# Square sums of 16 norms on four 32-column groups of the array, with their roots taken as rows

## The chip, the cores and the metric

The kernel runs on one core of a Trainium2 chip. The metric is the device time of one execution in microseconds; the kernel before took 1970.17 us (median of 3 runs, 1969.05 to 1970.89). One further execution was profiled. Engine names are those of the profile: PE is the matrix engine (PEld its weight loads), DVE, ACT and POOL are the vector, activation and general engines, SP issues the DMAs.

## The reference

A trunk of two layers over 1024 latent tokens of 1024 channels, with a context of 256 tokens. Layer 0 mixes tokens by a bidirectional recurrent block, layer 1 by a two-dimensional pooling mixer; each mixer is followed by a gated FFN with a convolution. Before and after each of these four blocks stands a norm over the channels of each token:

```python
def _rms_norm(x, g):
    xf = x.astype(jnp.float32)
    y = xf * lax.rsqrt(jnp.mean(xf * xf, axis=-1, keepdims=True) + EPS)
    return (y * g.astype(jnp.float32)).astype(x.dtype)
# per layer, latent stream:
h = _modulate(_rms_norm(x, norm_pre_mix[i]), sh_m, sc_m);  y = mixer(h)
x = x + g_m * _rms_norm(y, norm_post_mix[i])
f = _conv_ffn(_modulate(_rms_norm(x, norm_pre_ffn[i]), sh_f, sc_f), ...)
x = x + g_f * _rms_norm(f, norm_post_ffn[i])
```

So there are eight norms of the latent stream, four in each layer.

## The kernel before, in words

Everything lives transposed: channels on the 128 partitions in 8 tiles (KT), tokens along the free axis in two halves h of 512. The big products are made in three matmuls each, of high and low parts of both operands (line 803 and the lines 1221, 1249 and 1269 of the FFNs, which multiply two by two blocks with seven products and run in loops of ten steps); the two FFN loops fill most of the time. The order of each engine's work is written out by hand, and semaphores tie the engines together; an engine works strictly through its own list.

The norms are numbered q = 0 to 7 (even: before a mixer or FFN, odd: after it) and made for each half h, so there are 16. One norm goes like this:

1. ACT squares the eight channel tiles of a half (`square`). DVE or POOL add some of the squared tiles up beforehand (`chain_sums`, `even_sum`, `odd_sum`, `line_sums`); how many are left for PE is set by `form` and `chain_end`.
2. PE sums over the channels (`square_sums`, `direct_sums`, which call `column_sums`). For each of the four blocks t of 128 tokens the squares are the weights (128x128) and a column of ones streams past them, so the sums come out as columns, token on partition. The norms listed in `WIDE` stream 128 columns of ones instead of one, with 128 equal columns of sums. The calls per norm are (0,h): 1; (1,0): 1; (1,1): 2; (2,0): 1; (2,1): 4; (3,0): 1; (3,1): 3; (4,0): 5; (4,1): 1; (5,0): 1; (5,1): 4; (6,0): 4; (6,1): 5; (7,0): 1; (7,1): 3, in all 38.
3. ACT takes the root of the 128x4 sums into `rms` (`norm_root`).
4. DVE takes the reciprocal into `rstd` (`norm_scale`), four columns for each half.
5. PE spreads `rstd` over the partitions with four products against the identity (`spread`, not for q = 4, whose columns are used directly by `z_scale`), and DVE multiplies tiles by it from PSUM (`scale_tiles`, `gate`).

The norms 0 lie in the start, 1 and 2 around the second half of the first mixer's output product (`first_pair(0, ...)`), 3 at the end of the first FFN (`down_last`), 4 among the products with the pooling map (`z_tile`), 5 and 6 among and after the window sums and in `first_pair(1, ...)`, 7 at the end. PE's list puts other matmuls between steps 2 and 5, so that ACT and DVE have time for the root and the reciprocal:

```python
if (m, k) == (1, 3):
    square_sums(1, 0)
if (m, k) == (1, 7):
    spread(1, 0)
```

Of the kernel before, what the change touches and what calls it, by code (L numbers as in the profile page):

```python
# [19 lines left out]
P = 128  # L20
D = 1024
T = 1024
NC_ = 256
KT = D // P
# [42 lines left out]
FR = LINE / 1024  # L67
# [7 lines left out]
def build_trunk(nc, xT, ctxT, params, ada, wA, wB, wC, gatew, poolw, poolcnt, ident_in, outT):  # L75
    with ExitStack() as top:
# [7 lines left out]
        def overlay(*plan):  # L84
# [31 lines left out]
        ident = sb("ident", [P, P])  # L116
        ones = sb("ones", [P, P])
        eps = sb("eps", [P, 1])
        rms = sb("rms", [P, KT])
        rstd = sb("rstd", [P, KT])  # L120
        rms_c = sb("rms_c", [P, 2])
        rstd_c = sb("rstd_c", [P, 2])
# [9 lines left out]
            ("Hc_hi", [P, KT, NC_], F32R), ("Hc_lo", [P, KT, NC_], F32R), ("RA1", [P, TA]),  # L132
            ("IB0", [P, TA]), ("IB1", [P, TA]), ("TH0", [P, TA]), ("TH1", [P, TA]), ("gw", [P, 4, P]))
        RA, IB, TH = (RA0, RA1), (IB0, IB1), (TH0, TH1)
        quad, red = overlay(128 + FR, ("quad", [P, 4, D]), ("red", [P, 4, P]))
        sp, Mc, cAc = overlay(144 + FR, ("sp", [P, 8, 2 * NH]), ("Mc", [P, ADA0]), ("cAc", [P, KT]))
        ada_part, ada_row = overlay(56, ("ada_part", [P, 2, 4, P]), 2, ("ada_row", [P, 4 * P]))
# [215 lines left out]
        sq_made, sum_even, sum_odd = ([sem(f"{n}{h}") for h in range(2)] for n in ("sq_made", "sum_even", "sum_odd"))  # L353
        sum_both, sum_last = ([sem(f"{n}{h}") for h in range(2)] for n in ("sum_both", "sum_last"))
        zmap_made, z_scaled = sem("z_map_made"), sem("z_scaled")
        ssq_done, rms_made = ([sem(f"{n}{h}") for h in range(2)] for n in ("ssq_done", "rms_made"))
        rstd_made, rb_done = ([sem(f"{n}{h}") for h in range(2)] for n in ("rstd_made", "rb_done"))
        csq_made, ctx_norm_step = sem("ctx_sq_made"), sem("ctx_norm_step")
        caffine, chi, hc_ready = sem("ctx_affine"), sem("ctx_hi"), sem("ctx_h_ready")
# [145 lines left out]

            return 2 if q in (3, 7) else 6 + h if q == 4 else 4 + h

        WIDE = ((2, 1), (3, 1), (4, 0), (5, 1), (6, 0), (6, 1), (7, 1))

        def ssq_out(q, h):  # L510

            bank = ps[:, ssq_bank(q, h)]
            return bank if (q, h) in WIDE else bank[:, 4 * h:4 * h + 4]

        def rb_bank(q, h):

# [281 lines left out]
        def _(pe):  # L798
# [60 lines left out]

            def column_sums(q, h, src, at, first, last):  # L860

                out, w = ssq_out(q, h), P if (q, h) in WIDE else 1
                for t in range(4):
                    mm = pe.matmul(out[:, t * w:t * w + w], src[:, at + t * P:at + t * P + P],  # L864
                                   ones[:, 0:w], start=first and t == 0, stop=last and t == 3)
                if last:
                    mm.then_inc(ssq_done[h], 1)

# [44 lines left out]
                    pe.wait_ge(sum_last[h], trees_to(q + 1, h))  # L913
                    column_sums(q, h, *total, True, True)

            def shift_map(half):

                bank = 5 - half
                if half == 0:
                    pe.wait_ge(poolw_full, 16)  # L920
                    pe.wait_ge(coef_ready, 4)
                pe.wait_ge(d_added, half_added("22", 0, PAIRS) + (16 if half else 13))
                for g in (2 * half, 2 * half + 1):
                    for k in range(2):
                        c = (g % 2) * 512 + k * 256
                        mm = pe.matmul(ps[:, bank, (g % 2) * 256:(g % 2) * 256 + 256],
                                       M[:, 48 + 2 * g + k:49 + 2 * g + k].to_broadcast([P, P]),
                                       pool_w[:, half, c:c + 256], start=k == 0, stop=k == 1)
                mm.then_inc(z_done, 1)

            def spread(q, h):
# [5 lines left out]
                                   start=True, stop=True)  # L937
                mm.then_inc(rb_done[h], 1)

            def norm(q, h):  # L940
                square_sums(q, h)
                spread(q, h)


            def ada_rows(g, ks, units=slice(0, 4)):

# [36 lines left out]
            pe.wait_ge(const_full, 16)  # L983
            square_sums(0, 0)
            row_columns(0, 1, ada_cols)
            spread(0, 0)
            pe.wait_ge(ada_first_full[2], 32)
            ada_rows(1, range(KT))
# [17 lines left out]
            pe.wait_ge(ctx_norm_step, 5)  # L1006
            square_sums(0, 1)
            row_columns(3, 3, ada_out)
            first_pieces(0, pairs((4,)))
            spread(0, 1)  # L1010
            first_pieces(0, pairs((5, 6, 7)))
# [87 lines left out]
            for m in range(KT):  # L1099
                s, n = "AB"[m % 2], NH + REPEATED + m // 2  # L1100
                pe.wait_ge(w_ready[s], n + 1)
                pe.wait_ge(y_evac, m + 1 if m < 4 else m + 5)
                for k in range(KT):
                    if m == 0:
                        wait_gated(1, k)
                    if (m, k) == (1, 1):
                        pe.wait_ge(y_evac, KT)
                        ada_columns(4 * NH, 4, ps[:, 7, 0:4])
                    if (m, k) == (1, 3):
                        square_sums(1, 0)  # L1110
                    if (m, k) == (1, 7):
                        spread(1, 0)
                    if (m, k) == (5, 5):
                        square_sums(2, 0)
                    if (m, k) == (6, 1):
                        spread(2, 0)
                    mm = product(s, k * P, [(ps[:, m % 4], H_hi[:, k, hs(1)], H_lo[:, k, hs(1)])],
                                 k == 0, k == KT - 1)
                mm.then_inc(unit_done[s], 1)
# [33 lines left out]
            def down_last(L):  # L1153
# [21 lines left out]
                for n in range(6, 2 * KT):  # L1175
                    if n == KT:
                        pe.wait_ge(last_ready, 2 * L + 2)
                    pe.wait_ge(d_added, added + n - 5)
                    half_tile(n, False)
                    half_tile(n, True).then_inc(d_done, 1)  # L1180
                    if n == 8 and L == 0:
                        quad_columns(PAIRS + 1, ps[:, 3, 0:4])
                    if n == 10:
                        square_sums(q, 0)
                    if n == 11:
                        spread(q, 0)
                if L == 0:
                    shift_map(0)
                    square_sums(q, 1)
                    shift_map(1)  # L1190
                    spread(q, 1)
                else:
                    old_x(0, added + 12)
                    square_sums(q, 1)
                    old_x(2, added + 13)
                    spread(q, 1)
                    old_x(4, added + 14)
                    old_x(6, added + 15)
                    for m in TAIL_BANK:
                        plus_gated(m)  # L1200
# [81 lines left out]
            def first_pair(L, h):  # L1282
# [6 lines left out]
                for (s, banks), k in order:  # L1289
# [7 lines left out]
                    if (L, h, s) == (0, 0, "A"):  # L1297
                        if k == 0:
                            pe.wait_ge(y_evac, KT + 5)
                        if k == 3:  # L1300
                            square_sums(1, 1)
                        if k == 5:
                            spread(1, 1)
                    if (L, h, s, k) == (1, 0, "A", 4):
                        spread(5, 1)
                    if (h, s) == (0, "C"):
                        if (L, k) == (0, 0):
                            cols_and_second()
                        if (L, k) == (1, 2):
                            direct_sums(6, 1, KT - 2)  # L1310
                        if k == 3:
                            direct_sums(2 + 4 * L, 1, begin=KT - 2 if L else None)
                            square_sums(2 + 4 * L, 1, direct=False)
                        if k == 5:
                            spread(2 + 4 * L, 1)
                    mm = product(s, k * P, [piece(banks, H_hi, H_lo, k, h)], k == 0, k == KT - 1)
# [25 lines left out]

            ffn(0)

            def z_tile(i):

                b = 2 * (i % 3)
                if i == 0:
# [5 lines left out]
                for g in range(4):  # L1354
                    for k in range(2):
                        if i % 4 == 0:
# [2 lines left out]
                        mm = pe.matmul(ps[:, b + g // 2, (g % 2) * 256:(g % 2) * 256 + 256],  # L1359
                                       X[:, 2 * g + k, i * P:i * P + P], pool_s[:, g // 2, c:c + 256],  # L1360
                                       start=k == 0, stop=k == 1)
                mm.then_inc(z_done, 1)

            def window_sums(n):

                h, mt = n // KT, BOX_TILES[n]
                g, out = mt // 2, ps[:, n % 4]
# [20 lines left out]
                tiles.sort(key=lambda i: rows(i) != (8 * h, 8 * h + 8))  # L1388
                covered = 8 * h
                for i in tiles:  # L1390
                    r0, r1 = rows(i)
                    if n == 0 and i == KT - 1:
                        pe.wait_ge(zt_lo, KT)
# [14 lines left out]

            z_tile(0)
            square_sums(4, 0)  # L1410
            for i in range(1, 5):
                z_tile(i)
            square_sums(4, 1)
            for i in range(5, KT):
                z_tile(i)
            for n in range(2 * KT):
                window_sums(n)
                if n == 10:
                    square_sums(5, 0)
                if n == 11:  # L1420
                    spread(5, 0)
            square_sums(6, 0)
            spread(6, 0)
            square_sums(5, 1)
            ffn(1)
# [3 lines left out]
        def _(act):  # L1429
# [56 lines left out]

            def norm_root(q, h):
                act.wait_ge(ssq_done[h], q + 1)
                sums = ssq_out(q, h)
                if (q, h) in WIDE:  # L1490
                    sums = sums.rearrange("p (t c) -> p t c", t=4)[:, :, 0]
                A(rms[:, 4 * h:4 * h + 4], sums, ACT.Sqrt, scale=1.0 / D,
                  bias=eps[:, 0:1]).then_inc(rms_made[h], 1)

            def fill_h(i, L, ffn_part, h, ks=range(KT)):

# [918 lines left out]
        def _(dve):  # L2415
# [38 lines left out]

            def norm_scale(q, h):
                c = slice(4 * h, 4 * h + 4)
                dve.wait_ge(rms_made[h], q + 1)
                if q:
                    dve.wait_ge(rb_done[h], spreads_to(q))
                dve.reciprocal(rstd[:, c], rms[:, c]).then_inc(rstd_made[h], 1)  # L2460

            def ada_sum(i):

# [758 lines left out]
```

## Time and profile before

| | us |
|---|---|
| median of 3 runs | 1970.17 |
| profiled execution | 1970.25 |
| its span in the profile | 1968.4 |
| PE busy (98% of the span) | 1936.0 |
| DVE busy (85%) | 1664.5 |
| POOL busy (65%) | 1275.9 |
| ACT busy (51%) | 994.8 |

Matmuls overlap in the records: the time from one start to the next is what PE spends, not the length of a record. The profiled execution's time is 1.85 us longer than its span, which begins and ends with the first and last recorded work.

### The profile page before, as it was taken

Reading aid. Unit: us, or ns where it says so; the run is one execution under the profiler, and the core shown is the slowest. Engines: PE = TensorE matmul, PEld = TensorE weight load, DVE = VectorE, ACT = ScalarE, POOL = GpSimd, SP = SyncE. Lnnn points to the kernel's source line nnn. Section 1 sums busy time; section 2 is a strip of 40 time slices with the busy share of each in tenths; the row PEclk is TensorE's granted clock in tenths of the full one; section 3 lists DMA queues with packets and bytes.
Section 4 is the critical chain, followed back from the end, with each engine's and each line's share of the span. In section 5 each row is a group of like instructions: output and inputs, shape, how many; then the busy total and the mean of one; then the engine's idle time right before and its main releaser. Section 6 shows DMA issues by size and latency. Waiting matters only on the chain.

```text
span 1968.4 us, 28040 instructions
## 1 busy us (share of the span) xinstructions
PE 1936.0 (98%) x8830; PEld 1575.5 (80%) x8830; DVE 1664.5 (85%) x1760; ACT 994.8 (51%) x1423; POOL 1275.9 (65%) x856
## 2 busy tenths in 40 slices
PE   7999999999999999999999999999999999999999
PEld 3777777788888888888888789878888888888886
DVE  5588888878889898899889886897888888888887
ACT  5767768466544444444444465663433334333434
POOL 3544234575877788977788985475577655556765
PEclk9999999999999999999999999999999999999999
DMA  8232322541222223222232241111111111111114
GB/s 332 89 104 85 123 81 91 203 160 45 87 85 96 96 85 96 81 89 96 85 96 96 67 179 40 69 64 45 63 53 53 54 53 64 53 53 57 50 53 181
DMA packets 78016, 179.74 MB, mean 91 GB/s; under 512 B 5104, under 2 KB 28944, under 8 KB 77328
## 3 DMA queue, kind: packets, MB, share of 16 engines
q1 hardware_dynamic: 77968, 179.13, 26.6%
q8 instruction: 27, 0.44, 0.1%
q14 instruction: 21, 0.17, 0.0%
HBM read 166.52 MB, written 12.58 MB: 91 GB/s over the span
## 4 chain that ended last, share of the span: by engine, by line
PE 87%; DVE 5%; ACT 4%; POOL 2%; issue 1%; DMA 1%; SPq 1%; ACTq 0%; POOLq 0%; DVEq 0%
PE ps L1249 40%; PE ps L1269 19%; PE ps L803 17%; PE ps L1054 3%; PE ps L1398 2%; PE ps L864 1%; PE ps L1221 1%; DMA ada_first<-ada 1%; PE ps L1359 1%; DVE Y L2526 1%; PE ps L935 0%; DVE X L2536 0%; PE ps L857 0%; POOL rawC L2119 0%; ACT RA L1619 0%
## 5 line engine op out<-in xcount | busy, mean ns | idle before, releaser
L2303 POOL TENSOR_TENSOR So_lo<-So_raw,So_hi 128x512 fp32r<-128x512 f32 x120 | 197.8, 1656 | 199.2 <-DVE So_raw L2955 168.1
L3019 DVE TENSOR_TENSOR Y<-Y,ps 128x1024 f32<-128x1024 f32 x280 | 324.3, 1211 | 3.1
L1822 ACT ACTIVATE So_hi<-So_raw 128x512 fp32r<-128x512 f32 x180 | 112.4, 625 | 145.6 <-POOL So_raw L2295 73.0
L2074 POOL TENSOR_TENSOR red<-red,E_quad 128x512 f32<-128x512 f32 x77 | 123.4, 1603 | 61.5 <-ACT E_quad L1876 58.7
L1822 ACT ACTIVATE WB_hi<-rawB 128x512 fp32r<-128x512 f32 x120 | 74.6, 629 | 165.9 <-PE ps L1249 111.8
L2027 POOL TENSOR_TENSOR WA_lo<-rawA,WA_hi 128x1024 fp32r<-128x1024 f32 x20 | 58.0, 2899 | 144.2 <-DVE u L2648 103.6
L1822 ACT ACTIVATE WA_hi<-rawA 128x512 fp32r<-128x512 f32 x120 | 73.1, 625 | 123.2 <-PE ps L1269 83.4
L1249 PE MATMUL ps<-T_hi,So_hi 128*128 128x512 f32 x336 | 131.2, 391 | 0.0
L1249 PE MATMUL ps<-T_hi,So_lo 128*128 128x512 f32 x336 | 130.8, 389 | 0.0
L1249 PE MATMUL ps<-T_lo,So_hi 128*128 128x512 f32 x336 | 130.7, 389 | 0.0
L1249 PE MATMUL ps<-H_hi,WA_hi 128*128 128x512 f32 x336 | 130.7, 389 | 0.0
L1249 PE MATMUL ps<-H_lo,WA_hi 128*128 128x512 f32 x336 | 130.7, 389 | 0.0
L1249 PE MATMUL ps<-H_hi,WA_lo 128*128 128x512 f32 x336 | 130.7, 389 | 0.0
L2303 POOL TENSOR_TENSOR WB_lo<-rawB,WB_hi 128x512 fp32r<-128x512 f32 x80 | 128.9, 1630 | 0.0
L2303 POOL TENSOR_TENSOR WA_lo<-rawA,WA_hi 128x512 fp32r<-128x512 f32 x80 | 105.5, 1319 | 3.8 <-ACT WA_hi L1822 3.8
L3007 DVE TENSOR_TENSOR Ub<-t,ps 128x512 f32<-128x512 f32 x84 | 57.8, 688 | 46.6 <-ACT t L1854 37.9
L1726 ACT ACTIVATE S<-S 128x1024 f32<-128x1024 f32 x46 | 48.8, 1061 | 92.6 <-DVE S L2864 92.6
L803 PE MATMUL ps<-H_hi,WA_hi 128*128 128x512 f32 x252 | 91.0, 407 | 4.2 <-POOL WA_lo L2027 1.6
L2858 DVE SCALAR_TENSOR_TENSOR S<-Ub,par,S 128x1024 f32<-128x1024 f32 x48 | 83.7, 1744 | 6.2 <-ACT S L1721 6.2
L3007 DVE TENSOR_TENSOR t<-t,ps 128x512 f32<-128x512 f32 x84 | 57.3, 682 | 36.2 <-PE ps L1249 36.2
L803 PE MATMUL ps<-H_hi,WA_lo 128*128 128x512 f32 x252 | 87.3, 393 | 0.0
L803 PE MATMUL ps<-H_lo,WA_hi 128*128 128x512 f32 x252 | 87.2, 392 | 0.0
(450 smaller groups left out, 6299.4 us busy)
## 6 DMA issues: line engine op xcount, KB each, us to landing
rawA<-wA SPq DMA_DIRECT2D x62, 512.0 KB, 3.3
rawB<-wB SPq DMA_DIRECT2D x62, 512.0 KB, 3.3
E_quad<-ada SPq DMA_DIRECT2D x44, 512.0 KB, 3.4
quad<-ada SPq DMA_DIRECT2D x8, 2048.0 KB, 9.3
rawB<-wC SPq DMA_DIRECT2D x22, 512.0 KB, 3.7
rawA<-wC SPq DMA_DIRECT2D x20, 512.0 KB, 3.7
ada_first<-ada SPq DMA_DIRECT2D x8, 1024.0 KB, 15.6
outT<-X SPq DMA_DIRECT2D x16, 512.0 KB, 3.0
```

Source lines behind the costliest of these rows:

```text
L803: mm = pe.matmul(out, w[:, w_cols:w_cols + P], (hi, lo)[part], start=first and w is W_hi[s] and part == 0, stop=last and w is W_lo[s])
L1054: mm = pe.matmul(out, gw[:, gi], src, start=True, stop=True)
L1249: mm = pe.matmul(ps[:, UP_OUT[name]], w[:, at + k * P:at + k * P + P], right[part][:, k], start=k == 0 and w is hi and part == 0, stop=k = ...
L1269: mm = pe.matmul(ps[:, DOWN_OUT[name][m]], w[:, at + m * P:at + m * P + P], TOKEN[name][part], start=name in ("11", "S1", "12") and w is h ...
L1726: A(S[0][:], S[0][:], ACT.Gelu_apprx_tanh).then_inc(gelu_done, 1)
L1822: A(dst[:, at:at + HF], op_source(name), ACT.Copy).then_inc(op_hi, 1)
L2027: TT(W_lo[s][:], raw[s][:], W_hi[s][:].bitcast(F32), ALU.subtract).then_inc(w_ready[s], 1)
L2074: TT(red[:], red[:], E_quad[:, :, k % 2 * P:k % 2 * P + P], ALU.add).then_inc(red_made, 1)
L2303: TT(lo[:, at:at + HF], op_source(name), hi[:, at:at + HF].bitcast(F32), ALU.subtract)\
L2858: STT(S[0][:], Ub[:, 0:T], col("ffn_conv_w", 72 * L + j), S[0][:], ALU.mult, ALU.add)\
L3007: TT(dst, a, b, op).then_inc(up_added, 1)
L3019: TT(at, at, ps[:, bank:bank + 2, :], ALU.add).then_inc(d_added, 1)
```

## The change

The roles of squares and ones are swapped. Of each call the four token blocks go to the four groups of 32 columns of the array: the weights are 32 columns of ones, the squares of the block stream past (128 columns), and the sums come out as a row, on the 32 partitions of the block's group (32 equal rows). ACT takes the root of the whole 128x128 tile into a new SBUF tile `rms_row`. One new product, `root_columns`, has `rms_row` as weights and four columns of the identity (0, 32, 64, 96) as the moving operand; it gives the four columns of roots in the same PSUM bank, and DVE's reciprocal reads them there. `WIDE` is gone: all norms are done alike. `root_columns` stands in PE's list between the sums and the spread of each norm, at places chosen one by one: between two k tiles, inside `shift_map`, `z_tile` or `window_sums` (through a new argument `between`), or straight after the sums. One semaphore for each half, `rms_step`, counts both the root and the product. The number of calls of `column_sums` is the same.

```diff
-        def ssq_out(q, h):
-
-            bank = ps[:, ssq_bank(q, h)]
-            return bank if (q, h) in WIDE else bank[:, 4 * h:4 * h + 4]
+        def ssq_rows(q, h):
+
+            return ps[:, ssq_bank(q, h), 0:P]
+
+        def rms_columns(q, h):
+
+            return ps[:, ssq_bank(q, h), P:P + 4]
...
             def column_sums(q, h, src, at, first, last):
 
-                out, w = ssq_out(q, h), P if (q, h) in WIDE else 1
                 for t in range(4):
-                    mm = pe.matmul(out[:, t * w:t * w + w], src[:, at + t * P:at + t * P + P],
-                                   ones[:, 0:w], start=first and t == 0, stop=last and t == 3)
+                    mm = pe.matmul(ssq_rows(q, h)[32 * t:32 * t + 32], ones[:, 0:32], src[:, at + t * P:at + t * P + P],
+                                   start=first, stop=last)
...
+            def root_columns(q, h):
+
+                pe.wait_ge(rms_step[h], 2 * q + 1)
+                pe.matmul(rms_columns(q, h), rms_row[:], ident[:].rearrange("p (t c) -> p t c", t=4)[:, :, 0],
+                          start=True, stop=True).then_inc(rms_step[h], 1)
...
             row_columns(0, 1, ada_cols)
+            root_columns(0, 0)
             spread(0, 0)
...
             row_columns(3, 3, ada_out)
+            root_columns(0, 1)
             first_pieces(0, pairs((4,)))
...
                     if (m, k) == (1, 3):
                         square_sums(1, 0)
+                    if (m, k) == (1, 5):
+                        root_columns(1, 0)
...
+                    if (m, k) == (5, 7):
+                        root_columns(2, 0)
...
                     half_tile(n, False)
+                    if n == 11:
+                        root_columns(q, 0)
                     half_tile(n, True).then_inc(d_done, 1)
...
                     square_sums(q, 1)
-                    shift_map(1)
+                    shift_map(1, lambda: root_columns(q, 1))
                     spread(q, 1)
                 else:
                     old_x(0, added + 12)
                     square_sums(q, 1)
+                    root_columns(q, 1)
                     old_x(2, added + 13)
...
                         if k == 3:
                             square_sums(1, 1)
+                        if k == 4:
+                            root_columns(1, 1)
                         if k == 5:
                             spread(1, 1)
+                    if (L, h, s, k) == (1, 0, "A", 2):
+                        root_columns(5, 1)
                     if (L, h, s, k) == (1, 0, "A", 4):
                         spread(5, 1)
...
+                        if k == 4:
+                            root_columns(2 + 4 * L, 1)
                         if k == 5:
                             spread(2 + 4 * L, 1)
...
             square_sums(4, 0)
-            for i in range(1, 5):
+            z_tile(1, lambda: root_columns(4, 0))
+            for i in range(2, 5):
                 z_tile(i)
             square_sums(4, 1)
-            for i in range(5, KT):
+            z_tile(5, lambda: root_columns(4, 1))
+            for i in range(6, KT):
                 z_tile(i)
             for n in range(2 * KT):
-                window_sums(n)
+                window_sums(n, (lambda: root_columns(5, 0)) if n == 11 else None)
...
             square_sums(6, 0)
+            root_columns(6, 0)
             spread(6, 0)
...
             def norm_root(q, h):
                 act.wait_ge(ssq_done[h], q + 1)
-                sums = ssq_out(q, h)
-                if (q, h) in WIDE:
-                    sums = sums.rearrange("p (t c) -> p t c", t=4)[:, :, 0]
-                A(rms[:, 4 * h:4 * h + 4], sums, ACT.Sqrt, scale=1.0 / D,
-                  bias=eps[:, 0:1]).then_inc(rms_made[h], 1)
+                A(rms_row[:], ssq_rows(q, h), ACT.Sqrt, scale=1.0 / D, bias=eps[:, 0:1]).then_inc(rms_step[h], 1)
...
-                dve.wait_ge(rms_made[h], q + 1)
+                dve.wait_ge(rms_step[h], 2 * q + 2)
                 if q:
                     dve.wait_ge(rb_done[h], spreads_to(q))
-                dve.reciprocal(rstd[:, c], rms[:, c]).then_inc(rstd_made[h], 1)
+                dve.reciprocal(rstd[:, c], rms_columns(q, h)).then_inc(rstd_made[h], 1)
```

## Rows read from the trace of the kernel before

**Rows 1.** The page: busy time of the engines, and the chain that ended last.
```profile
PE 1936.0 (98%) x8830; PEld 1575.5 (80%) x8830; DVE 1664.5 (85%) x1760; ACT 994.8 (51%) x1423; POOL 1275.9 (65%) x856
...
PE 87%; DVE 5%; ACT 4%; POOL 2%; issue 1%; DMA 1%; SPq 1%; ACTq 0%; POOLq 0%; DVEq 0%
```
**Rows 2.** The chain of waits from 380 to 470 us, then 1130 to 1300: shares by line.
```profile
by line: PE ps L803 82.1%; PE ps L864 7.6%; PE ps L935 4.0%; PE ps L850 1.5%; POOL H_lo L2038 1.5%; DVE Y L2512 0.8%; ACT H_hi L1501 0.8%; ACT H_hi L1505 0.7%; ACT Y L1503 0.7%; PE ps L1278 0.4%; issue 0.3%; ACTq L1498 0.0%
...
by line: PE ps L1398 18.8%; PE ps L803 10.3%; PE ps L1359 8.4%; PE ps L864 8.1%; issue 7.4%; PE ps L1380 3.6%; DVE X L2536 2.9%; DVE T_raw L2836 2.7%; DVE V L2423 2.6%; DVE T_raw L2838 2.5%; DVE Y L2526 2.4%; POOL X L2084 2.2%; ACT H_hi L15
```
**Rows 3.** PE's groups by shape, line 864: xcount | busy us, mean ns | idle before.
```profile
L864 PE MATMUL ps<-ones,sq 128*128 128x128 f32 x104 | 12.2, 276 | 0.0
...
L864 PE MATMUL ps<-ones,sq 128*128 128x1 f32 x32 | 3.7, 242 | 0.0
```
**Rows 4.** Windows of line 864: stretch and length, busy (xcount), granted clock, DMA share, GB/s.
```profile
0.00:1968.00 1968.00, 37.29 (x304) 1.00 0.27 91
...
1163.80:1168.34 4.54, 4.54 (x40) 4.51 (x39) 1.00 0.00 0
...
387.19:388.00 0.81, 0.81 (x8) 0.81 (x7) 1.00 0.00 0
```
**Rows 5.** PE's timeline around small products: start us, length us, line, operands, xcount [idle before].
```profile
440.36 0.39 PE L803 MATMUL ps<-H_hi,WB_lo 128*128 128x512 f32 x1
440.68 0.40 PE L1278 MATMUL ps<-ident,cnt_row 32*128 32x32 f32 x2
441.01 0.60 PE L850 MATMUL ps<-ones,red 128*128 128x1 f32 x4
...
36.34 4.45 PE L950 MATMUL ps<-ada_first,silu_c 128*2 128x512 f32 x10 [1.87 <-DMA ada_first<-ada]
40.73 0.50 PE L803 MATMUL ps<-H_hi,WA_hi 128*128 128x512 f32 x1
```
**Rows 6.** Windows of all engines: PE, PEld, DVE, ACT, POOL busy (xcount), then granted clock.
```profile
50.00:52.00 2.00, 0.52 (x3) 0.55 (x3) 0.74 (x1) 1.23 (x3) 1.93 (x2) 0.83 0.00 0
...
50.00:60.00 10.00, 8.52 (x35) 7.74 (x36) 6.28 (x11) 7.15 (x14) 7.45 (x6) 0.66 0.56 168
...
1234.00:1238.00 4.00, 4.00 (x37) 3.97 (x36) 3.30 (x6) 2.19 (x4) 3.55 (x3) 1.00 0.42 161
```
**Rows 7.** ACT's groups by shape: the roots, and a copy of 128x512 out of PSUM.
```profile
L1492 ACT ACTIVATE rms<-ps,eps 128x4 f32<-128x4 f32 x16 | 4.1, 258 | 23.4 <-PE ps L864 23.4
...
L1960 ACT ACTIVATE z_shift<-ps 128x512 f32<-128x512 f32 x2 | 1.2, 598 | 0.4 <-PE ps L926 0.4
```
**Rows 8.** Timeline of the norms (1,1) and (2,1), all engines.
```profile
431.15 0.18 DVE L2460 RECIPROCAL rstd<-rms 128x4 f32<-128x4 f32 x1 [0.35 <-ACT rms L1492]
...
445.06 0.69 DVE L2445 TENSOR_TENSOR sq<-ps,sq 128x512 f32<-128x512 f32 x1
...
447.40 0.27 ACT L1492 ACTIVATE rms<-ps,eps 128x4 f32<-128x4 f32 x1 [4.31 <-PE ps L864]
...
452.17 0.47 PE L803 MATMUL ps<-H_hi,WA_hi 128*128 128x512 f32 x1 [0.47 <-DVE H_lo L2518]
```
**Rows 9.** Timeline of the norms (3,1), (4,0), (5,0), (6,0) and (5,1), all engines.
```profile
1158.22 0.18 DVE L2460 RECIPROCAL rstd<-rms 128x4 f32<-128x4 f32 x1 [0.76 <-ACT rms L1492]
...
1165.55 1.74 POOL L2055 TENSOR_TENSOR sq<-sq 128x512 f32<-128x512 f32 x1
...
1220.12 0.24 ACT L1492 ACTIVATE rms<-ps,eps 128x4 f32<-128x4 f32 x1
...
1235.72 0.69 DVE L2445 TENSOR_TENSOR sq<-ps,sq 128x512 f32<-128x512 f32 x1
...
1245.66 0.18 DVE L2460 RECIPROCAL rstd<-rms 128x4 f32<-128x4 f32 x1 [0.51 <-ACT rms L1492]
```
**Rows 10.** Timeline of the tail, norm (7,1): DVE's adds and ACT's root.
```profile
1954.25 2.62 DVE L2536 TENSOR_TENSOR X<-X,Y 128x512 f32<-128x512 f32 x2
...
1956.52 0.26 ACT L1492 ACTIVATE rms<-ps,eps 128x4 f32<-128x4 f32 x1 [2.18 <-PE ps L864]
```

More of the change, by code:

```diff
@@ L118, in build_trunk @@
         eps = sb("eps", [P, 1])
-        rms = sb("rms", [P, KT])
+        sb("gap_rms", [P, KT])
         rstd = sb("rstd", [P, KT])
@@ L134, in build_trunk @@
         RA, IB, TH = (RA0, RA1), (IB0, IB1), (TH0, TH1)
+        rms_row, = overlay(145 + FR, ("rms_row", [P, P]))
         quad, red = overlay(128 + FR, ("quad", [P, 4, D]), ("red", [P, 4, P]))
@@ L355, in build_trunk @@
         zmap_made, z_scaled = sem("z_map_made"), sem("z_scaled")
-        ssq_done, rms_made = ([sem(f"{n}{h}") for h in range(2)] for n in ("ssq_done", "rms_made"))
+        ssq_done, rms_step = ([sem(f"{n}{h}") for h in range(2)] for n in ("ssq_done", "rms_step"))
         rstd_made, rb_done = ([sem(f"{n}{h}") for h in range(2)] for n in ("rstd_made", "rb_done"))
@@ L506, in ssq_bank @@
             return 2 if q in (3, 7) else 6 + h if q == 4 else 4 + h
-        WIDE = ((2, 1), (3, 1), (4, 0), (5, 1), (6, 0), (6, 1), (7, 1))
-        def ssq_out(q, h):
-            bank = ps[:, ssq_bank(q, h)]
-            return bank if (q, h) in WIDE else bank[:, 4 * h:4 * h + 4]
+        def ssq_rows(q, h):
+            return ps[:, ssq_bank(q, h), 0:P]
+        def rms_columns(q, h):
+            return ps[:, ssq_bank(q, h), P:P + 4]
         def rb_bank(q, h):
@@ L914, in square_sums, with shift_map @@
                     column_sums(q, h, *total, True, True)
-            def shift_map(half):
+            def shift_map(half, between=None):
                 bank = 5 - half
@@ L928, in shift_map @@
                                        pool_w[:, half, c:c + 256], start=k == 0, stop=k == 1)
+                    if g % 2 == 0 and between is not None:
+                        between()
                 mm.then_inc(z_done, 1)
@@ L938, in spread @@
                 mm.then_inc(rb_done[h], 1)
-            def norm(q, h):
-                square_sums(q, h)
-                spread(q, h)
+            def root_columns(q, h):
+                pe.wait_ge(rms_step[h], 2 * q + 1)
+                pe.matmul(rms_columns(q, h), rms_row[:], ident[:].rearrange("p (t c) -> p t c", t=4)[:, :, 0],
+                          start=True, stop=True).then_inc(rms_step[h], 1)
             def ada_rows(g, ks, units=slice(0, 4)):
@@ L1343, in _, with z_tile @@
             ffn(0)
-            def z_tile(i):
+            def z_tile(i, between=None):
                 b = 2 * (i % 3)
@@ L1361, in z_tile, with window_sums @@
                                        start=k == 0, stop=k == 1)
+                    if g == 0 and between is not None:
+                        between()
                 mm.then_inc(z_done, 1)
-            def window_sums(n):
+            def window_sums(n, between=None):
                 h, mt = n // KT, BOX_TILES[n]
@@ L1390, in window_sums @@
                 for i in tiles:
+                    if i == tiles[len(tiles) // 2] and between is not None:
+                        between()
                     r0, r1 = rows(i)
```

## The prediction

> **What bounds the kernel now.** I read the page first, then the chain of waits in the two stretches where most norms lie, then the records of the square sums, then the timeline around each norm. The page shows a kernel bound by TensorE: PE is busy 98% of the span and makes 87% of the chain that ended last [rows 1]. The change touches the 16 norms only (8 places q, two token halves h), and 12 of them lie in two stretches near the middle, around the mixers. There the chain is not PE's alone: from 380 to 470 us the square sums (L864) are 7.6% of it, some 6.8 us, and from 1130 to 1300 us 8.1%, 13.8 us, with DVE, POOL and ACT in between [rows 2]. So at most some 20 us are in play, and only where PE is what ends last.
>
> **What is there now.** Column_sums is called 38 times: 304 records, 37.3 us busy, so 152 matmuls of two records each (fp32 makes two passes) [rows 4]. Ten calls stream 1 column, 28 stream 128 (a group of each in [rows 3]; the four wide groups have 104, 64, 40 and 16 records). A block of five wide calls lasts 4.54 us, 0.1135 a record and 0.91 a call; a narrow call lasts 0.81 [rows 4]. In all 28 x 0.91 + 10 x 0.81 = 33.6 us of PE's queue.
>
> **Part 1, the sums on 32-column groups.** Still four matmuls of two records, each now streaming 128 columns past a 32-column weight. No row has this form. If the four groups run one after another, eight records at 0.1135 make 0.91 a call: no gain, and 0.10 lost on the ten narrow ones. If all four run side by side, two passes remain: 0.23. Between them lies what I take: PE starts its records in order, and the two passes of one matmul use the same 32 columns, so the second waits for the first; only the second pass of one block and the first of the next can overlap. That is four steps, 4 x 0.1135 = 0.45 a call and one step of 0.11 more for a run of calls: 0.57 for one, 2.38 for five instead of 4.54. A wide record lasts 276 ns and starts 0.1135 us after the one before [rows 3, 4]: in this trace only the tail of one overlaps the next. The Trainium skill (TensorE: Matmul & The Clock Gate, Part 3: Packing small matmuls) lets matmuls on different column groups run at the same time, each starting some 4 ns after the last. No row here has two at once; by that rule a call would be the 0.23 of all four side by side, and the time that of rival B.
>
> **Part 2, changing the shape of the array.** A small product with 32 rows between full ones: it starts 0.32 us after the last full matmul where the next full one would come 0.23 after (0.23 is the step of the big stream), and its two records last 0.33 instead of 0.20 (two of the 0.10 that a record of the narrow calls takes) [rows 5]. So about 0.2 a visit. The row with two weight columns agrees roughly: ten records of 512 columns fill 4.39 us up to the next full matmul, 0.44 each where two cycles of 2.4 GHz a column would make 0.43, so 0.1 is the most that leaving can have cost there [rows 5]. I take 0.2 for each of the 17 runs of calls, bounds 0.1 and 0.3: 3.4 us.
>
> **Part 3, the product back to columns.** Sixteen new matmuls of two records each: 0.20 by the narrow calls, 0.33 by the small product in the stream [rows 4, 5], 0.25 taken, 4 us. So PE's own account is 38 x 0.45 + 17 x 0.31 + 4 = 26.4 against 33.6: 7 us less. One after another it is 34.6 + 3.4 + 4 = 42, 8 more; all side by side 8.7 + 3.4 + 4 = 16, 17 less.
>
> **Part 4, a longer chain in each norm.** ACT's root grows from 128x4 (0.26) to 128x128; a 128x512 read of PSUM is 0.60, so 0.34 between them by size, +0.08 [rows 7]. The root then goes through PE's queue: at least 0.4 us (two records and their latency), and as long as PE's work ahead of it lasts. DVE's reciprocal waits for that, and behind it on DVE stand the gates and scalings of the next tiles. So each norm gives 0.5 us back on DVE wherever DVE stood waiting for the root.
>
> **What of it lies on the path, place by place** (side-by-side pairs, 0.45):
> - Norms (0,0) and (0,1), in the start: 0. PE waits 1.87 us for a DMA soon after the first [rows 5]; the second gains in the sums what the root product takes.
> - (1,0) and (2,0), one call each in PE's stream: 0.57 + 0.2 + 0.25 - 0.81 = +0.2 each. (1,1), two calls: 1.02 + 0.2 + 0.25 - 1.62 = -0.15, but DVE's reciprocal already waited for ACT [rows 8] and now waits for PE too: +0.35, and the gates follow it. (2,1), four calls: -1.6 in the sums, of which the last must wait for DVE's chain of adds, ready at 445.75 (445.06 + 0.69) while the root starts at 447.40 [rows 8]: the sums can end 0.8 sooner, the root product gives 0.4 back, and the 0.35 is lost before. After it PE waits for DVE anyway (0.47 [rows 8]). Together -0.1.
> - (3,0) starts on a DVE add and goes back to the stream at the same time: 0. (3,1), three calls: -0.9, of which DVE can use 0.5, since it stood 0.76 waiting for this root [rows 9]. (4,0), five calls: -1.9 on PE, but its total comes from POOL, at 1167.29 (1165.55 + 1.74), and the block ended at 1168.34 [rows 4, 9]; POOL follows DVE, so the 0.5 stays and no more. (4,1): +0.15.
> - (5,0) lies between window sums, where PE is the bound. ACT's root comes at 1220.12, behind other ACT work [rows 9], and PE meets the root product at about 1220.0, so it stands until 1220.45: +0.4 with the rest.
> - (6,0): its total is ready at 1236.41 (1235.72 + 0.69) [rows 9]; the block of four ran to 1238.17, now to 1237.0; root and product give 0.4 back, and PE stands twice where it stood once: -0.5 after the shift from (5,0). (5,1): the sums save 1.3, but its root product stands in PE's queue behind two k tiles, and DVE's reciprocal, which waited 0.51 [rows 9], waits some 0.35 more, with the scalings and then the gates behind it. (6,1): -0.4. Together -0.55.
> - (7,0), (7,1): 0. In the tail DVE's adds run to 1956.87 (1954.25 + 2.62), past the root at 1956.52 [rows 10]; sums that end 1.3 sooner meet a DVE that is not free.
>
> The sum is -0.1 - 0.5 + 0.15 + 0.4 - 0.55 = -0.6 us. The big loops between 500 and 1100 and between 1300 and 1930 have none of it. The profiled execution took 1970.25 (span 1968.4 and 1.85 around it), 0.08 above the median of the runs, so 1969.6 in either.
>
> **Rivals.** A: the four groups don't overlap, slower. Each place pays the toll, the product and the longer chain and gets nothing: layer 0's mixer +2.0 (PE arrives 1.0 late at (1,1), whose two calls, root and product add 0.85, and DVE's gates carry it to (2,1)), layer 1's +3.4 (0.8 at (3,1), 0.4 in (4,1), 0.9 at (5,0), 0.6 at (6,0), 0.5 at (5,1), 0.2 at (6,1)), the tail +0.6: +6, 1976.2. It decides once a call costs more than about 0.6 us; for it speaks that no matmul in this trace runs beside another. B: all four side by side, 0.23 a call: PE has 17 us less, but the totals from DVE and POOL and the waits of DVE named above are the same; the places give -0.5, -0.8 and, around (6,0) to (6,1), -0.9: some -2, 1968.2. This is the case that the page named in part 1 describes. C: the clock. PE was busy for only 0.52 of the 2 us from 50 to 52, and over 50 to 60 the granted clock was 0.66 in the mean, which is 6.8 of 10 us at 1.2 GHz instead of 2.4; the dense wide sums from 1234 to 1238 kept it at 1.00 [rows 6]. With sums of half the length and more standing between 1234 and 1243 it may fall there. Half such a stretch, or a whole one, filled with matmuls at half speed costs 1.7 to 3.4 us; less the 0.6, about 1972.
>
> **How the numbers follow.** Forecast 0.46, A 0.22, B 0.20, C 0.12. About 0.2%, 3.9 us, is what a measurement can tell from no change: below 1966.2 counts as faster, above 1974.1 as slower. Faster are a seventh of the forecast's cases (its places gain more than worked out) and a third of B's: 0.13. Slower are nine tenths of A's and a sixth of C's: 0.22. The range runs from 1966.5 (B with one more us) to 1976.8 (A); the forecast's own is 1967.5 to 1972.
>
> **What would show it.** Right: weights of 32 columns, a call's eight records in 0.45 to 0.57 us, the second record of a block and the first of the next starting almost together; the sums (L864's line) about 17 us from start to end in all; sixteen small products; PE's waits for ACT's root at (5,0) and (6,0); DVE's waits before the reciprocals longer; the mixers' stretches of the same length within 1 us. Wrong: eight records evenly 0.11 apart (A), four starts within 0.02 (B), a granted clock under 1 near 1240 (C), or a total more than 4 us from before.

## The result, and the profile after

The changed kernel takes 1974.1 us (median of 16 runs, 1971.87 to 1976.61), the kernel before 1970.13 in the same runs: ratio 1.0017, 95% interval [1.0011, 1.0024]. It is 3.4 us slower by the ratio, 4.0 by the medians. The forecast was 1969.6, with 1967.5 to 1972 as its own range. The profiled execution took 1974.46, its span is 1972.7 (+4.3).

The page of the changed kernel, busy time of the engines (beside [rows 1]), and under it PE's groups at the sums (line 865 now), the root product (946) and ACT's root (1515): count | busy, mean ns | idle before.

```profile
PE 1927.8 (98%) x8862; PEld 1553.5 (79%) x8862; DVE 1667.3 (85%) x1760; ACT 996.0 (50%) x1423; POOL 1278.2 (65%) x856
```
```profile
L865 PE MATMUL ps<-sq,ones 128*32 128x128 f32 x136 | 6.0, 288 | 6.3 <-DVE sq L2467 3.3 <-POOL sq L2077 2.8
L946 PE MATMUL ps<-ident,rms_row 128*128 128x4 f32 x32 | 5.9, 255 | 2.6 <-ACT rms_row L1515 2.4
```
```profile
L1515 ACT ACTIVATE rms_row<-ps,eps 128x128 f32<-128x128 f32 x16 | 5.7, 358 | 15.1 <-PE ps L865 15.1
```

PE has 8.2 us less to do and yet ends later. The wide groups of `sq` had no idle time ahead of them [rows 3]; the new ones have 6.3 us, in which PE waits for DVE and POOL to finish the squares.

Windows of line 865 alone in the changed kernel: the whole span, then four calls of (4,0). PE and PEld busy (xcount), granted clock.

```profile
0.00:1972.00 1972.00, 14.79 (x304) 7.54 (x304) 0.99 0.27 91
1162.30:1163.40 1.10, 1.08 (x32) 0.81 (x32) 1.00 0.00 0
```

14.8 us instead of 37.3 [rows 4], and four calls in 1.08 where five took 4.54. The sums became far shorter than I forecast. What came of that, at (4,0), all engines of the changed kernel in order of time (idle before and its releaser in brackets):

```profile
1162.30 1.08 PE L865 MATMUL ps<-sq,ones 128*32 128x128 f32 x32
...
1164.45 1.72 POOL L2077 TENSOR_TENSOR sq<-sq 128x512 f32<-128x512 f32 x1
...
1166.22 0.66 PE L865 MATMUL ps<-sq,ones 128*32 128x128 f32 x8 [2.85 <-POOL sq L2077]
...
1166.81 2.08 PE L1378 MATMUL ps<-pool_s,X 128*128 128x256 f32 x4
...
1168.96 5.34 PE L1378 MATMUL ps<-pool_s,X 128*128 128x256 f32 x15
```

The fifth call cannot begin before POOL's total. Before, PE streamed ones during that time (1163.80 to 1168.34 [rows 4]); now it stands for 2.85 us, and the pooling products behind it take 0.43 us from start to start (1169.53 to 1171.24 for four of them), where they took 0.22. The windows of the changed kernel (PE, PEld, DVE, ACT, POOL busy, then granted clock) show why, here and at two more places:

```profile
1160.00:1166.00 6.00, 3.38 (x43) 2.54 (x42) 6.00 (x9) 2.97 (x5) 5.86 (x4) 0.99 0.00 0
1166.00:1172.00 6.00, 5.78 (x21) 4.45 (x22) 5.87 (x7) 2.66 (x5) 6.00 (x6) 0.50 0.01 3
...
1241.00:1244.00 3.00, 3.00 (x36) 2.68 (x39) 1.59 (x3) 1.95 (x3) 0.00 (x0) 0.50 0.01 3
1264.00:1268.00 4.00, 3.15 (x15) 2.38 (x16) 0.88 (x3) 0.37 (x1) 0.00 (x0) 0.61 0.24 93
```

TensorE's clock is granted at 1.2 instead of 2.4 GHz from 1165.9 to 1172.7, 1241.0 to 1244.4 and 1264.9 to 1268.3: 13.7 us. The kernel before has one such stretch between 100 and 1950 us, 3.4 us at 348, and none in these places. The same view of it:

```profile
1160.00:1166.00 6.00, 6.00 (x41) 5.59 (x40) 6.00 (x7) 3.44 (x7) 5.86 (x5) 1.00 0.00 0
1166.00:1172.00 6.00, 6.00 (x39) 5.57 (x38) 6.00 (x8) 2.74 (x6) 6.00 (x5) 1.00 0.01 3
...
1241.00:1244.00 3.00, 3.00 (x27) 2.91 (x26) 2.35 (x4) 2.77 (x5) 0.70 (x1) 1.00 0.00 0
```

To see where the time went I took matmuls that both traces have and subtracted their start times. The table gives how much later PE is than in the kernel before, with zero at 395 us, behind norm (1,0). (At 395 the start and the stretch at 348 have left 0.28.) Two of the experiments stand beside it.

| at (before) | behind | changed | filled (fill_three) | 4, 5, 6 as before (late_old) |
|---|---|---|---|---|
| 500 | norms 1, 2 | -0.64 | -0.59 | -0.63 |
| 1150 | (3,0) | -0.41 | -0.57 | -0.29 |
| 1163 | (3,1) | -1.87 | -2.04 | -1.75 |
| 1171 | (4,0) | +1.31 | -0.95 | -1.29 |
| 1219 | (4,1) | +0.06 | -2.09 | -1.27 |
| 1233 | (5,0) | +1.38 | -0.77 | -1.27 |
| 1260 | (6,0), (5,1) | +1.75 | -0.71 | -1.28 |
| 1272 | (6,1) | +3.74 | -0.24 | -1.29 |
| 1964 | norm 7 | +4.03 | -0.23 | -1.16 |

Up to 1163 the change pays, 1.9 us. From there it loses 5.9: 3.2 at (4,0), of which 1.25 comes back by 1219; 1.3 at (5,0); 0.4 around (6,0) and (5,1); 2.0 at (6,1); 0.3 in the tail. At (5,0) the clock is at 1.00. PE's, ACT's and DVE's timelines there, changed kernel:

```profile
1220.13 0.33 PE L1421 MATMUL ps<-band,ZT_lo 128*128 128x256 f32 x1
1221.27 0.39 PE L946 MATMUL ps<-ident,rms_row 128*128 128x4 f32 x2 [0.81 <-ACT rms_row L1515]
1221.52 0.42 PE L1421 MATMUL ps<-band,ZT_hi 128*128 128x192 f32 x2
```
```profile
1220.17 0.80 ACT L2012 ACTIVATE Y<-Y,pbs,par 128x512 f32<-128x512 f32 x1
1220.87 0.34 ACT L1515 ACTIVATE rms_row<-ps,eps 128x128 f32<-128x128 f32 x1
```
```profile
1221.69 0.18 DVE L2482 RECIPROCAL rstd<-ps 128x4 f32<-128x4 f32 x1 [1.62 <-PE ps L946]
```

ACT's root has other work of ACT ahead of it and PE, the bound here, stands 0.81 us for it in the middle of the window sums; DVE's reciprocal waits 1.62, where it waited 1.07 for ACT.

### The profile page after: what moved, and what is told of

Read it like the earlier page. It is cut to its first block and busy times, and to the rows that moved or that the text cites. A ratio compares the mean times of both kernels' runs of the same rounds, so it can differ in the third digit from the quotient of the medians.

```text
span 1972.7 us, 28108 instructions
## 1 busy us (share of the span) xinstructions
PE 1927.8 (98%) x8862; PEld 1553.5 (79%) x8862; DVE 1667.3 (85%) x1760; ACT 996.0 (50%) x1423; POOL 1278.2 (65%) x856
## 5 line engine op out<-in xcount | busy, mean ns | idle before, releaser
L2096 POOL TENSOR_TENSOR red<-red,E_quad 128x512 f32<-128x512 f32 x77 | 123.4, 1603 | 61.5 <-ACT E_quad L1898 58.6
```

The costliest lines, as they stand in the source:

```text
L2096: TT(red[:], red[:], E_quad[:, :, k % 2 * P:k % 2 * P + P], ALU.add).then_inc(red_made, 1)
```

## The experiments

Theory: the sums are so short that PE stands where it streamed ones before, the clock falls, and the matmuls behind run at 1.2 GHz. Rival: the longer chain (root, PE's queue, product, reciprocal) is what costs, and the clock only fills time in which PE would wait. Each kernel ran with the kernel before on the same chip. "At 0.50" is the time at 1.2 GHz between 100 and 1950 us in the profiled execution.

| run | median us | ratio to before, 95% | at 0.50 |
|---|---|---|---|
| changed | 1974.1 | 1.0017 [1.0011, 1.0024] | 13.7 |
| fill_one | 1971.44 | 1.0004 [0.9995, 1.0013] | 3.4 |
| fill_all | 1970.47 | 0.9998 [0.9989, 1.0007] | 0 |
| fill_three | 1970.28 | 0.9999 [0.9990, 1.0008] | 0 |
| late_old | 1968.79 | 0.9991 [0.9983, 1.0000] | 0 |
| before_narrow | 1987.45 | 1.0083 [1.0070, 1.0095] | 44 |
| narrow_40 | 1972.44 | 1.0007 [0.9998, 1.0017] | 3.4 |
| old_50 | 1971.9 | 1.0010 [1.0001, 1.0019] | 13.7 |
| group_fill | 1969.51 | 0.9998 [0.9989, 1.0007] | 10.2 |
| mixed_fill | 1970.61 | 0.9997 [0.9988, 1.0006] | 10.2 |
| mixed | 1968.96 | 0.9995 [0.9986, 1.0004] | 3.4 |
| before_start | 1969.15 | 0.9996 [0.9987, 1.0005] | 3.4 |
| late_start | 1967.08 | 0.9986 [0.9977, 0.9995] | 3.4 |

**Products that nobody reads, in PE's stands** (fill_one, fill_all, fill_three).

```diff
+            def fill(bank, n):
+                for i in range(n):
+                    pe.matmul(ps[:, bank, 256:384], ones[:], ident[:], start=True, stop=True)
...
+                    if (q, h) == (4, 0):
+                        pe.wait_ge(zmap_made, KT + 2)
+                        fill(4, 11)
                     pe.wait_ge(sum_odd[h], odds_to(q + 1, h))
```


> The changed kernel, and in the norm (4,0) eleven plain products of 128x128 (ones by the identity, into a bank that nobody reads) in PE's list between the fourth call of the sums and the wait for POOL's total, where PE stands 2.85 us in the changed kernel and the clock then falls for 6.8 us. They fill about 2.5 us of the stand. Theory (the clock): the granted clock stays 1.00 from 1160 to 1175, the pooling products step by 0.22 instead of 0.43, and of the 3.1 us that they lost some 1 to 2 reach the end, since PE waits for DVE and ACT a little later anyway: about 1972.5 against 1974.1. Rival (the longer chain through PE's queue is what costs, the clock only fills time in which PE would wait): the clock may stay up, the time stays within 0.5 of the changed kernel's.

> The same eleven products at (4,0), seven more at (6,0) before the last call of the sums (PE stands 1.88 us there), four before the first sums of (6,1) (1.23 us) and four before its last (1.07 us). Theory (the clock): no stretch at 0.50 from 1160 to 1270, all of the 10 us of half speed that the changed kernel has more than the one before is gone, worth 3 to 4.5 us: about 1970.2, the kernel before's time. Rival (the longer chain): at most 1 us less than the changed kernel, 1973 or more.

> The run with filling products at (4,0), (6,0) and twice at (6,1) again; the last four products now go into a bank that no other product uses at that time. Theory (the clock): no stretch at 0.50 from 1160 to 1270, 3 to 4 us less than the changed kernel: 1970 to 1971. What is then left against the kernel before is the longer chain: PE 1.3 late at (5,0) and some 0.4 at (6,1), against 1.5 early after (3,1).

In fill_all the last four products overwrite a bank in which a product of the FFN still stands; fill_three is the same without that. Timeline of PE in fill_three at (4,0), and its windows:

```profile
1161.79 1.08 PE L865 MATMUL ps<-sq,ones 128*32 128x128 f32 x32
1162.81 2.72 PE L873 MATMUL ps<-ident,ones 128*128 128x128 f32 x22
1165.72 0.42 PE L865 MATMUL ps<-sq,ones 128*32 128x128 f32 x8 [0.19 <-POOL sq L2090]
```
```profile
1166.00:1172.00 6.00, 5.34 (x32) 4.38 (x25) 5.87 (x7) 3.15 (x6) 6.00 (x5) 1.00 0.00 0
...
1241.00:1244.00 3.00, 1.94 (x14) 1.12 (x14) 2.67 (x5) 2.77 (x5) 1.17 (x1) 1.00 0.00 0
1264.00:1268.00 4.00, 3.52 (x20) 2.79 (x19) 2.58 (x4) 1.90 (x3) 0.00 (x0) 1.00 0.00 0
```

The stand of 2.85 is 0.19, and the clock stays at 1.00 in all three places. Twenty-six useless matmuls more make the kernel 3.8 us faster (3.5 by the ratios, whose intervals don't meet). That is the theory's number; the rival had 1 at most. By the table, the clock cost 2.0 at (4,0), 0.3 around (6,0) and 1.5 at (6,1). With one filling alone, at (4,0), some two thirds of it is back (1.0004 against 1.0017, with intervals that overlap); its profile still has 3.4 us at 0.50 near 1238.

The profiles are of one execution each, but the mean granted clock of all runs goes the same way: 0.9936 for the changed kernel, 0.9962 for fill_three, 0.9965 for late_old, and 0.9964 for the kernel before in the 29 runs beside late_old. The filling does not hold the clock in every execution: the runs of fill_three go from 1967.23 us at 0.998 to 1974.39 at 0.994.

**Streaming one column instead of 128 in the kernel before** (before_narrow, narrow_40): `WIDE = ()`, and `WIDE` without (4,0).

> The kernel before with one streamed column in all 38 calls (no wide sums); nothing else is changed. PE's list is hardly shorter (0.81 instead of 0.91 a call, 2.8 us in all) and PE stands about as before, but a call streams 8 columns instead of 1024. If the clock is held up by what is streamed, it falls to 0.50 near 1166 and near 1240 as in the changed kernel and the time is 2 to 4 us longer: about 1973. If only standing counts, the clock stays 1.00 there and the time is 1969 to 1970.

> The kernel before with one streamed column instead of 128 in the five calls of the norm (4,0) alone; nothing else is changed, and PE's list keeps its length there (0.81 instead of 0.91 a call). If the wide sums of this one norm hold the clock up, a stretch at 0.50 of 3.4 or 6.8 us begins near 1166 to 1172 and none near 1241 and 1265; it costs 1 to 2 us: 1971 to 1972.5. Rival (the 17 us of the kernel with all calls narrow come from many small stands, not from what one norm streams): clock 1.00 from 1160 to 1180 and the same time as before.

before_narrow, windows of all engines as above:

```profile
1250.00:1260.00 10.00, 10.00 (x34) 8.57 (x35) 5.68 (x9) 7.16 (x12) 4.25 (x4) 0.57 0.00 0
...
1270.00:1280.00 10.00, 10.00 (x49) 9.27 (x49) 3.51 (x6) 1.53 (x3) 1.27 (x1) 0.61 0.27 105
```

narrow_40, the same view, then PE's timeline:

```profile
1160.00:1166.00 6.00, 6.00 (x42) 5.59 (x41) 6.00 (x7) 3.45 (x7) 5.86 (x5) 1.00 0.00 0
1166.00:1172.00 6.00, 6.00 (x32) 5.29 (x32) 6.00 (x8) 2.74 (x7) 6.00 (x5) 0.74 0.01 3
```
```profile
1163.76 4.58 PE L864 MATMUL ps<-ones,sq 128*128 128x1 f32 x40
1168.21 7.98 PE L1359 MATMUL ps<-pool_s,X 128*128 128x256 f32 x28
```

This takes the chain out of the question: no row, no root product, and PE busy 6.00 of 6.00 us. The block of five calls is as long as before (4.45 us from its start to the next product, 4.54 before), but streams single columns; the clock falls behind it in this execution, from 1168.9 to 1172.3, PE loses 1.7 us, and 0.8 of it is left at 1290. The measured time of narrow_40 does not settle it alone: its interval holds 1, and the granted clocks of its runs (0.993 to 0.997) are close to those of the kernel before beside it (0.994 to 0.997; one run of each, of several ms, is left out). With all calls narrow it is 17 us, far more than I expected (3), and all six runs have a mean granted clock of 0.984 to 0.987. So the wide sums kept the clock up in this kernel; behind the narrow ones of narrow_40 it fell although PE was busy all the time.

**The norms 4, 5 and 6 in the form before** (late_old), and less (old_50, mixed). In each, `column_sums`, `norm_root` and `norm_scale` choose the form by a list:

```diff
+        OLD = ((4, 0), (4, 1), (5, 0), (5, 1), (6, 0), (6, 1))
...
+                    if (q, h) in OLD:
+                        out, w = ssq_out(q, h), P if (q, h) in WIDE else 1
+                        mm = pe.matmul(out[:, t * w:t * w + w], src[:, at + t * P:at + t * P + P],
+                                       ones[:, 0:w], start=first and t == 0, stop=last and t == 3)
+                        continue
```


> The changed kernel with the norms 4, 5 and 6 of both halves in the form before (squares as weights, wide sums for (4,0), (5,1), (6,0), (6,1), root of 128x4, no root product); norms 0, 1, 2, 3 and 7 stay on the column groups. Both theories expect the loss to go; the numbers differ in what is left of the gains: in the changed kernel PE is 0.4 us early after the norms 1 and 2 and 1.5 us early after (3,1). If PE bounds what follows, 1968.5 to 1969; if POOL and DVE set the end of (4,0), only the 0.4 and some tenths stay: 1969.5. Clock 1.00 from 1160 to 1270.

> The changed kernel with the norm (5,0) alone in the form before (one streamed column, root of 128x4, no root product). In the changed kernel, and in both runs with filling products alike, PE goes from 0.3 late to 1.6 late (against the kernel before) at this norm's root product, where it stands 0.81 for ACT's root. If that stand is a loss of its own, the loss at this place is gone and the time is 1 to 1.3 less than the changed kernel's: about 1973, with the clock stretches near 1166, 1241 and 1265 still there. Rival (the stand only takes time that PE would lose a little later): 1974.

> Column groups for the norms 0, 1, 2 and (3,1) alone, nothing filled, all others in the form before. Against the run with the norms 4, 5 and 6 in the form before, (3,0) and the tail give up another 0.3 each: 1968 to 1968.5, clock 1.00 from 1160 to 1270. Rival: the same 1968.8 as that run.

late_old gains the same 1.8 us up to 1163, has 1.3 of it left at 1171 and loses next to nothing after that: 1.9 less than before by the medians, though the interval touches 1. old_50 loses nothing at (5,0) (PE's lateness changes by 0.00 between 1219 and 1233, +1.32 in the changed kernel), and its ratio lies 1.4 us under that of the changed kernel as expected, with intervals that overlap: the loss at (5,0) is shown in the trace, not in the time. The clock still falls near 1168 and 1240. mixed has (3,0) and the tail in the form before too and was expected at 1968 to 1968.5; it took 1968.96, and nothing in its time tells it from late_old, as its rival had it.

**Both causes together** (group_fill: groups for all but (5,0), filled as in fill_three; mixed_fill: a choice by place).

> Column groups for all norms but (5,0), with the filling products at (4,0), (6,0) and (6,1). The run with these products and all norms on groups took 1970.3, and PE lost 1.3 us in it at (5,0). If both causes add up, 1969; no stretch at 0.50 from 1160 to 1270. Rival (what PE gains at (5,0) it loses in its waits for DVE around (6,0)): 1970.3 as without.

> Column groups for the norms 0, 1, 2, (3,1), (4,0) and (6,0), with filling products at (4,0) (eleven) and (6,0) (seven); the form before for (3,0), (4,1), (5,0), (5,1), (6,1), (7,0), (7,1). Worked out from PE's place against the kernel before in the runs so far: about -0.4 at norm 1, -0.6 at norm 2, -1.5 at (3,1), 0 at (4,0), 0 at (5,0), -0.6 at (6,0), 0 after: some 2.5 to 3 us less than before, 1967.5 to 1968. Rival (what PE gains early is lost in its waits for POOL and DVE): 1969 to 1970.

group_fill comes 0.8 under fill_three and near its expected 1969; the ratios can't tell them apart. mixed_fill is a miss of some 3 us. In both profiles the clock fell for 3.4 us near 349, 448 and 1147, where the same instructions ran at 1.00 in fill_three. Each of these two profiles is of the slowest of its 11 runs, so they show what slowed that run and not the median. Why the clock fell there and not in the others stays open.

**A stand that has nothing to do with the change** (before_start, late_start): five filling products near 33 us, eight near 50 (the eight are shown).

```diff
             pe.wait_ge(ctx_norm_step, 5)
+            fill(5, 8)
             square_sums(0, 1)
```


> The kernel before with filling products (128x128, ones by the identity, into a bank that is free) at two stands of PE in the start that have nothing to do with the change: five ahead of the wait for the squares of the context near 33 us, eight ahead of the sums of (0,1) near 50 us, after which the clock is at 0.50 for 6.8 us in nearly every profile so far. If a stand filled with products holds the clock up in general, the stretch near 53 to 60 is gone and the time is 1 to 2.5 us less than before: 1968 to 1969.5. Rival (in the start DMA and POOL set the pace): same as before within 0.5.

> The same two fillings of the start in the kernel with column groups for the norms 0 to 3 and 7 and the form before for 4, 5 and 6. If gains add up: 1.9 less for the norms and 1 to 2.5 for the start, 1966.3 to 1967.8. Rival as above: 1968.8.

late_start, PE's timeline, and the windows of late_old, which lacks the filling, and of late_start itself:

```profile
48.98 2.05 PE L886 MATMUL ps<-ident,ones 128*128 128x128 f32 x16
51.25 0.43 PE L878 MATMUL ps<-rawC,ones 128*32 128x128 f32 x8 [0.22 <-POOL rawC L2170]
```
```profile
52.00:56.00 4.00, 4.00 (x23) 3.40 (x24) 2.96 (x8) 3.91 (x8) 4.00 (x4) 0.63 0.65 143
56.00:60.00 4.00, 4.00 (x15) 3.48 (x15) 3.02 (x4) 3.88 (x7) 3.09 (x3) 0.52 0.83 323
```
```profile
52.00:56.00 4.00, 3.95 (x25) 3.46 (x26) 3.76 (x9) 3.94 (x8) 4.00 (x4) 1.00 0.78 213
56.00:60.00 4.00, 3.83 (x17) 2.87 (x16) 3.13 (x4) 3.90 (x8) 3.12 (x3) 1.00 1.00 377
```

The fall of 6.8 us is gone in late_start; in before_start half of it is left (55.1 to 58.6), and its gain alone, 0.9, is not certain. One profile can't show that the filling did it: fill_all has no filling in the start, PE stood there as well, and in its profiled execution the clock stayed up:

```profile
48.00:52.00 4.00, 1.69 (x8) 0.24 (x8) 1.36 (x3) 3.64 (x7) 3.71 (x4) 1.00 0.00 2
52.00:56.00 4.00, 4.00 (x32) 3.46 (x32) 3.81 (x8) 3.49 (x7) 4.00 (x4) 1.00 0.60 144
```

All runs together speak for the filling: the mean granted clock is 0.9979 in late_start for 0.9965 in late_old, and 0.9972 in before_start for 0.9963 in the kernel before. late_start is the one version that beats both kernels beyond its interval: 3.0 us less than before by the medians, 2.8 by the ratio.

## Why the prediction was wrong

- **Part 1 failed.** It let only the second pass of one block overlap the first of the next: 0.45 a call. All four run side by side: at (4,0) the first four records start 0.007 us apart, the next four 0.11 later; four calls take 1.02 us from their start to the next matmul (1161.79 to 1162.81 in fill_three), 0.25 each, and 0.22 after the first. This is the lower bound, rival B's. The Trainium skill (TensorE: Matmul & The Clock Gate, Part 3: Packing small matmuls), by which matmuls on different column groups start some 4 ns apart, was nearer than the rows on which I settled; the trace has 7.
- **Parts 2 to 4 held.** At (5,0) PE goes from the last full product to the next in 0.56 us with the sums between (1219.07 to 1219.63): 0.11 the usual step of such a matmul, 0.24 the call, 0.21 the changes of shape; before it was 0.98 (1218.31 to 1219.29). The root product takes 0.25 (1221.27 to 1221.52). The root takes 0.36 for 0.34.
- **The gains** were forecast as 0.1 in layer 0 and 0.5 at (3,1), and are 0.6 and 1.5. The 0.6 is near rival B's 0.5. At (3,1) the forecast was wrong in the wait too: it counted only what DVE could use of the shorter sums, but PE was busy for 8.00 of the 8 us from 1155 to 1163 in the changed kernel, so PE set the pace there and its saving came through.
- **"POOL follows DVE, so the 0.5 stays and no more", at (4,0), and the like at (6,0) and (6,1).** Here the prediction lost the time. I counted PE's stand as free, because PE waits for somebody else in any case. It isn't free: behind it the matmuls run at half speed. PE loses 3.2 us at (4,0), 2.0 of it by the clock when set against fill_three, and 2.0 at (6,1), 1.5 of it by the clock. I had this as rival C, but priced at one place (1234 to 1243), with half a stretch or one; there were three, the first where I had not looked, 13.7 us in all. And I held B and C apart with a chance for each, when B makes C: the shorter the sums, the longer the stand.
- **(5,0)** was +0.4 and is 1.3. I placed the end of PE's stand by the root of the kernel before, at 1220.45; the root began 0.75 later, because ACT was late by as much behind DVE, while PE's last full matmuls were 0.36 late (1220.13 for 1219.77).
- **(6,1)** was -0.4; with the clock at 1.00 it still costs 0.5 (fill_three), and no run was made on why. The tail was 0 and is +0.3 in this profile, but 0.0 in fill_three with the same instructions there, so no cost of the tail is shown.
- The measured 1974.1 lies between 1966.5 and 1976.8 by luck: the upper end came from rival A, whose mechanism (the four groups don't overlap) the trace refutes.
- Signs that I had named: the four starts within 0.02 us (B) and the clock under 1 near 1240 (C) are both there.

## What to carry to other kernels

A matmul whose time looks wasted may be paying for the clock of those behind it: before PE's work is shortened ahead of a wait, ask what PE will do during that wait, and read the granted clock in the windows behind it. A stand that can't be removed can be filled with products that nobody reads. And work that moves an engine's result through the bound engine's queue is put where that result is already there, not in the middle of its stream.

## What the runs showed of the hardware that I had not expected

- The clock fell with PE busy all the time (the profiled execution of narrow_40: 6.00 of 6.00 us, granted clock 0.74 in the next window), when what PE did was to load 128x128 weights and stream one column past each.
- The same program does not always fall at the same places. The 16 runs of the changed kernel go from 1971.87 us at a mean granted clock of 0.995 to 1976.61 at 0.991. before_start, whose norms are all in the form before, had a stretch of 3.4 us at 1144 that cost it 1.6.
- Of two adds of 128x512 that run together, either can be the one that takes longer. DVE's and POOL's timelines near (6,0), first the kernel before, then the changed one:

```profile
1233.32 0.69 DVE L2445 TENSOR_TENSOR ps<-sq 128x512 f32<-128x512 f32 x1
```
```profile
1232.88 2.26 POOL L2084 TENSOR_TENSOR X<-X,Y 128x512 f32<-128x512 f32 x1 [0.84 <-DVE Y L2526]
```
```profile
1234.97 1.78 DVE L2467 TENSOR_TENSOR ps<-sq 128x512 f32<-128x512 f32 x1
```
```profile
1234.52 1.67 POOL L2106 TENSOR_TENSOR X<-X,Y 128x512 f32<-128x512 f32 x1 [0.83 <-DVE Y L2548]
```

In the one POOL's add takes 2.26 and DVE's 0.69, in the other 1.67 and 1.78, and DVE's is in the chain of the norm. No run was made on it.
